# Two 128-column value products instead of three 64-column ones in a softmax attention branch, and eleven filler products left out

## Chip, cores and metric

One NeuronCore of a Trainium2 chip runs the whole program. The metric is the device time of one execution in microseconds (us). TensorE does the matrix products, VectorE (DVE), ScalarE (ACT) and GpSimd (POOL) the elementwise work; SyncE (SP) issues the large loads. All data are fp32; most products run on operands that were split into a high and a low part in the 32-bit matmul format (`F32R`).

## The reference, cut to what matters

Two transformer blocks on 512 tokens, width 1024. The first block mixes a retention branch with a softmax branch (`nsa`) of 8 query heads in 2 groups of keys and values, head width 64. The second block has two SwiGLU layers, a stick-breaking attention, a chunked softmax attention and a last gated projection.

```python
def nsa(q, kv_all, gate_logits, pos, ...):
    k_c, v_c, k_s, v_s, k_w, v_w = [kv[:, :, i] for i in range(6)]
    ...
        p_cmp = masked_softmax(s, cmp_end[None, :] <= tq[:, None])
        o_cmp = jnp.einsum('bghqn,bgnd->bghqd', p_cmp, vcT)          # compressed
        ...
        o_slc = jnp.einsum('bghqm,bgqmd->bghqd', p_slc, vg)          # selected
        ...
        o_win = jnp.einsum('bghqk,bgkd->bghqd', p_win, vwb)          # window
    o = g[..., 0:1] * o_cmp + g[..., 1:2] * o_slc + g[..., 2:3] * o_win
```

With 512 tokens the selection takes every block and the window covers all, so the selected and the window part are plain causal softmax attentions with keys and values of their own.

## The kernel before

**High and low parts.** A value a is kept as AH, its rounding to the matmul format, and AL = a - AH. `mm3` (lines 277 to 279) makes a product of two such values from three matmuls: high x low of the moving side, high x high, low x high. It takes three operand pairs and sums into one PSUM bank; the low x low part is left out.

**The softmax branch.** `NSA_UNITS` has 64 units: 8 heads, two kinds (selected, window) and 4 blocks of 128 queries, i = 0 to 3. A unit with block i sees (i + 1) blocks of 128 keys. `softmax_pairs` takes two units at a time (s = 0, 1; heads j and j + 4) in steps m, in the order of blocks 0, 3, 0, 3, 1, 2, 1, 2 for each head pair j, so 8 steps make a round and 4 rounds the branch. In step m TensorE does, in this order:

- the scores of pair m (L1646, three products per unit, the two units side by side in the upper and lower 64 rows) and the causal mask (L1720, a bf16 product with the identity),
- the transposes of the softmax weights of pair m - 3 (L1730), once GpSimd has scaled them (`sc`) and the bank is free (`lo` of the pair before),
- the value products of pair m - 4 into the banks B0 and B1 (`mm3`, L277 to L279): the values `VNH`, `VNL` (64 columns) are the loaded operand, the transposed weights `AH2`, `AL2` (128 columns) are streamed.

ScalarE takes the exponentials and rounds the transposed weights (`AH<-B`), VectorE takes the row maxima (L1248), the low parts (L1260) and reciprocals (L1266). A round collects one head pair in B0 and B1. At its end (m = 12, 20, 28, 36) ScalarE copies 64 rows of each bank to T10, T11 (event `at_x`, printed `T<-B 64x512`), and `nsa_first` begins the next round in the same banks with the compressed values `BD` (L1759), which waits for `at_x`. After two rounds (m = 20, 36) VectorE multiplies T10, T11 with the gate (`at_m`, L1273), ScalarE rounds (`at_hi`), VectorE takes the low part (`at_lo`, L1278).

**Behind it.** The output projection "p2" begins on TensorE right after the last value product; its weights are split on ScalarE (`KEPT_H`, L560) and VectorE (`KEPT_L`, L1021). In VectorE's queue some of these splits stand behind the `at_m` and `at_lo` of m = 36 and 37.

**Stick-breaking.** `stick_breaking(n)`, n = 4 to 38, is a pipeline over 32 units. At even n TensorE waits for a bank, runs `keep_clock` (L1528: matmuls of 128x512 on `VAH` whose result nobody reads), then the scores of two units (L1646); at every n it does the sums of later terms (`sb_later_sums`, L1866) once VectorE has made their low part, and the values of unit n - 7. `keep_clock` runs 10, 10 and 6 products at n = 4, 6 and 8, one at n = 10 to 30, and 6 at n = 32 and 34.

Of the kernel before, what the change touches and what calls it, by code (L numbers as in the profile page):

```python
# [17 lines left out]
P = 128  # L18
# [4 lines left out]
HD = 64  # L23
# [18 lines left out]
F32R = mybir.dt.float32r  # L42
# [22 lines left out]
def build(nc, a):  # L65
    with ExitStack() as ctx:
# [24 lines left out]
        def hb(name, kb, shape, dt=F32):  # L91
            return at(name, OFF_H + kb * KB, shape, dt)
# [8 lines left out]
        DECAY = hb("DECAY", 48, [P, NH, SEQ])  # L101
        QNH, QNL = hb("QNH", 64, [P, 4, SEQ], F32R), hb("QNL", 72, [P, 4, SEQ], F32R)
        KNH, KNL = hb("KNH", 80, [P, 2, SEQ], F32R), hb("KNL", 84, [P, 2, SEQ], F32R)
        VNH, VNL = hb("VNH", 88, [P, 4, 256], F32R), hb("VNL", 92, [P, 4, 256], F32R)
        Y_H = hb("Y_H", 48, [P, KT, SEQ])
        MRH, MRL = hb("MRH", 0, [P, 4, SEQ], F32R), hb("MRL", 8, [P, 4, SEQ], F32R)
        GR = hb("GR", 16, [P, 4, SEQ])
# [3 lines left out]
        W2K = hb("W2K", 52, [P, 2, 2, P])  # L111
        W2V = hb("W2V", 54, [P, 2, HD])
        HV4 = hb("HV4", 55, [P, 2, 2, 4, 32])
        BD = hb("BD", 57, [P, 2, 4, HD])
        KCF = hb("KCF", 59, [P, 4, 32])

        KPH, KPL = hb("KPH", 48, [P, 4, P], F32R), hb("KPL", 50, [P, 4, P], F32R)
        SCT = at("SCT", OFF_U + 4 * KB, [P, 2, SEQ])
# [172 lines left out]
            "pt_hi pt_lo pp ep pl_s".split())}  # L291


        pl_y, at_x, at_m, at_hi, at_lo = (Event(n) for n in "pl_y at_x at_m at_hi at_lo".split())
        f_g, f_s, f_u, f_h, f_hh, f_hl = (sem(n) for n in "f_g f_s f_u f_h f_hh f_hl".split())
        NSA = {n: Event("nsa_" + n) for n in "s max exp rec sc tr hi lo pv".split()}
        BAND = {n: Event("", NSA[n], 64) for n in "s max exp rec sc tr hi lo pv".split()}
# [59 lines left out]
        def nsa_unit(h, kind, i):  # L357
            g, j, L = h // 4, h % 4, (i + 1) * P
            rows, cols = slice(64 * g, 64 * g + 64), slice(i * P, (i + 1) * P)
            o = slice(kind * P + g * HD, kind * P + (g + 1) * HD)  # L360
            return {"h": h, "i": i, "L": L, "q": (QNH[rows, j, cols], QNL[rows, j, cols]),
                    "k": (KNH[rows, kind, 0:L], KNL[rows, kind, 0:L]), "mask": MASKB[:, 0, :], "bias": None,
                    "gate": GLS[:, i, 3 * h + kind + 1:3 * h + kind + 2],
                    "v": lambda b: (VNH[:, b, o], VNL[:, b, o])}

        def band_unit(h, i):
            L = (i + 1) * P
# [188 lines left out]
        def _(act):  # L556
# [100 lines left out]
            for d in range(32):  # L657
                if 4 <= d + 2 < 32:
                    hi_of_weights(d + 2)
                if d in ROT_DONE:  # L660
                    r = ROT_DONE[d]
                    wait(act, E["q_rot"], r + 1)
                    dst, scale = ROT_HI[r]
                    E["q_hi"].mark(f(dst, T[10][:, :], ACT.Copy, scale=scale))
                if d == 14:
                    wait(act, E["angle"], 2)
                    E["sines"].mark(f(T[2][:, :], T[3][:, :], ACT.Sin, scale=0.5))
                    wait(act, E["sines"], 3)
                    E["sines"].mark(f(T[3][:, :], T[3][:, :], ACT.Sin))
                act.wait_ge(mm, d + 1)  # L670
                kind = P1_KIND[d]
                bank = B[uses["p1", d][0]] if kind != TOK else None
                if kind == ROT:
                    wait(act, E["q_rot"], P1_ROT[d] - 3)
                    for q in range(4):
                        here, other = slice(32 * q, 32 * q + 32), slice(32 * (q ^ 1), 32 * (q ^ 1) + 32)
                        ins = f(Q_RING[P1_ROT[d] % 4][here, :], bank[other, :], ACT.Copy)
                    E["q_swap"].mark(ins)
                elif kind == GATE:
                    E["gates"].mark(f(RG[:, d // 16, d % 4, :], bank[:, :], ACT.Silu))  # L680
                elif kind == TOK and d % 4 == 3:
                    for t in range(TT):
                        if d < 16:
                            E["v_hi"].mark(f(VRH[:, t, :], B[4 + t][:, :], ACT.Copy))
                        else:
                            f(GLS[:, t, :], B[4 + t][:, 256:280], ACT.Sigmoid)
                            E["v_hi"].mark(f(VNH[:, t, :], B[4 + t][:, 0:256], ACT.Copy))


            for m in range(25):  # L690
# [198 lines left out]
            n = 0  # L889
# [121 lines left out]
        def _(dve):  # L1011
# [97 lines left out]
            for d in range(32):  # L1109
# [23 lines left out]
                if kind == CMP:  # L1133

                    dve.wait_ge(mm, d + 1)
                    kv = d - 20
                    bank = B[uses["p1", d][0]]
                    for g in range(2):
                        rows = slice(64 * g, 64 * g + 64)
                        tok = bank[rows, :].rearrange("p (n r) -> p r n", r=16)  # L1140
                        for l2 in range(2):
                            for part in range(2):
                                pe = PE2[rows, kv, 16 * part + l2:16 * part + 16:2]
                                ins = tt(FC[kv][64 * l2:64 * l2 + 64, 8 * part:8 * part + 8, g, :],
                                         tok[:, l2:16:2, part:part + NC],
                                         pe.unsqueeze(2).broadcast_to([64, 8, NC]), ALU.add)
                                E["k_flat"].mark(ins)
                elif kind == TOK and d % 4 == 3:
                    for t in range(TT):
                        wait(dve, E["v_hi"], (4 if d > 16 else 0) + t + 1)  # L1150
                        if d < 16:
                            E["v_lo"].mark(tt(VRL[:, t, :], B[4 + t][:, :], VRH[:, t, :], ALU.subtract))
                        else:
                            E["v_lo"].mark(tt(VNL[:, t, :], B[4 + t][:, 0:256], VNH[:, t, :], ALU.subtract))

            def compressed_keys_values():

                wait(dve, E["cmp_kv"], 1)
                for g in range(2):
                    rows = slice(64 * g, 64 * g + 64)  # L1160
                    tt(KCF[rows, 1, 0:NC], B[6][rows, g * NC:(g + 1) * NC], T[2][rows, NC:SEQ:16], ALU.mult)
                    chain.done(tt(KCF[rows, 2, 0:NC], B[6][rows, 64 + g * NC:64 + (g + 1) * NC], T[3][rows, NC:SEQ:16], ALU.mult))
                    chain.done(tt(KCF[rows, 0, 0:NC], KCF[rows, 1, 0:NC], KCF[rows, 2, 0:NC], ALU.add))
                for j in range(4):
                    cols = slice(32 * j, 32 * j + 32)
                    E["cmp_kh"].mark(v.tensor_copy(KPH[:, j, cols], KCF[:, 0, :]))
                wait(dve, E["cmp_kh"], 4)
                for j in range(4):
                    cols = slice(32 * j, 32 * j + 32)
                    E["cmp_kl"].mark(tt(KPL[:, j, cols], KCF[:, 0, :], KPH[:, j, cols], ALU.subtract))  # L1170
                for g in range(2):
                    for j in range(4):
                        rows = slice(32 * j, 32 * j + 32)
                        E["cmp_bd"].mark(v.tensor_copy(BD[rows, g, j, :], B[6][rows, P + HD * g:P + HD * (g + 1)]))


            dve.wait_ge(decay_here, 16)
            for m in range(26):
# [21 lines left out]
                if m == 17:  # L1200
# [3 lines left out]
                    v.memset(BD[:, :, :, :], 0.0)  # L1204
                    chain.done(v.memset(HV4[:, :, :, :, :], 0.0))
                    for KP in (KPH, KPL):
                        chain.done(v.tensor_copy(KP[:, :, :], BD[:, :, :, :].rearrange("p g j e -> p (g j e)").rearrange("p (j c) -> p j c", j=4)))
                    for hf in range(2):
                        src = HIDT[:, 1, hf, :].rearrange("p (g n) -> p g n", g=2).unsqueeze(2).broadcast_to([P, 2, 4, NC])
                        E["cmp_dup"].mark(v.tensor_copy(HV4[:, hf, :, :, 0:NC], src))  # L1210
# [55 lines left out]
                            tag["rec"].mark(v.reciprocal(RECS[:, u % 8:u % 8 + 1], SUMS[:, u % 8:u % 8 + 1]))  # L1266

            def nsa_ahead(m):
                if m in (20, 36):
                    for s in range(2):  # L1270
                        p = m // 36 + 2 * s
                        wait(dve, at_x, 4 * (m // 36) + 3 + s)
                        at_m.mark(tt(T[10 + s][:, :], T[10 + s][:, :], RG[:, 1, p, :], ALU.mult))  # L1273
                if m in (21, 37):
                    for s in range(2):
# [222 lines left out]
        def _(pe):  # L1498
# [209 lines left out]
            def softmax_pairs(units, tag, ahead, first):  # L1708

                N = len(units) // 2  # L1710
                for m in range(N + 4):
# [20 lines left out]
                    if m >= 4:  # L1732
                        for s in range(2):
# [3 lines left out]
                            started = first(m - 4, s)  # L1737
                            wait(pe, tag["lo"], u + 1)
                            for b in range(i + 1):
                                ins = mm3(B[s][0:HD, i * P:(i + 1) * P], *x["v"](b), AH2[:, u % 4, b * P:(b + 1) * P],  # L1740
                                          AL2[:, u % 4, b * P:(b + 1) * P], b == 0 and not started, b == i, skip_group_check=True)
                            tag["pv"].mark(ins)
# [12 lines left out]

            def nsa_first(m, s):
                if m % 8 == 0:
                    wait(pe, at_x, 2 * (m // 8 - 1) + s + 1)
                    mat(B[s][0:HD, :], BD[:, s, m // 8, :], PTC[:, s, :], start=True, stop=False, skip_group_check=True)  # L1759
                return True  # L1760

            wait(pe, E["gn_ln"], 4)
# [38 lines left out]
            def mlp_down(phase, d0, t, hidden):  # L1801
# [14 lines left out]
                for n in range(16):  # L1816
# [5 lines left out]
                    for k in range(FT - 16):  # L1822
# [8 lines left out]
            wait(pe, E["gn_lo"], 4)  # L1831
            project_out("p2", D_P2, 0, lambda k: MRH[:, k, :] if k < 4 else UH[:, k, :],
                        lambda k: MRL[:, k, :] if k < 4 else UL[:, k, :],
                        bank_free=lambda m: wait(pe, *((NSA["exp"], 62), (NSA["exp"], 62), (at_x, 7), (at_x, 8), (NSA["lo"], 64), (NSA["exp"], 64))[m]),
                        then=lambda: None,
                        ready=lambda k: wait(pe, at_lo, {4: 1, 5: 3, 6: 3, 7: 4}[k]))
            mlp_up("f1", D_F1, 0, 0)
# [80 lines left out]
            def stick_breaking(n):  # L1918
                if n < SB_ALONE and n % 2 == 0:
                    if n >= 8:  # L1920
                        wait(pe, E["sb_p"], n - 4)
                    else:
                        wait(pe, E["p5_vlo"], n + 2)
                    keep_clock({4: 10, 6: 10, 8: 6}.get(n, 1 if n < 32 else 6), VAH[:, 0, :], sb_bank(n))
                    if n < 32:
                        sb_scores(n)
                if SB_EARLY <= n - 3 < 32:
# [162 lines left out]
```

## Time and profile before

| | |
|---|---|
| time, median of 3 runs | 1579.76 us (1579.65 to 1583.11) |
| profiled execution: its own time | 1579.92 us |
| profiled execution: span | 1578.2 us |
| mean granted TensorE clock | 0.982 |
| TensorE busy | 1488.9 us (94%), 8593 matmuls |
| softmax branch, steady part | about 311 to 386 us |
| steady stick-breaking | about 972 to 1018 us |

The span is what the trace covers; the execution's own time lies 1.7 us above it. Busy time is a sum over instructions; matmuls overlap, so a busy TensorE can still be one that waits between short pieces. PEld is TensorE's loading of the operand that stays in the array. The granted clock is 1.00 at 2.4 GHz and 0.50 at 1.2 GHz. "Idle" in brackets is the time that an engine stood still just before an instruction, with what ended it.

### The profile page before, as it was taken

What the parts mean: (1) busy time and instruction counts of PE and PEld (TensorE: products, weight loads), DVE (VectorE), ACT (ScalarE), POOL (GpSimd) and SP (SyncE); (2) the same over time, 40 slices, a digit from 0 to 9 for tenths busy, and PEclk for the clock granted to TensorE, in tenths of its full rate; (3) what the DMA queues carried; (4) which work ended last, traced back from release to release, by engine and by line L of the source; (5) the groups of instructions that cost most, each with busy time, mean ns of one, the idle gap of its engine ahead of it and who ended that gap; (6) DMA issues with size and microseconds to landing.
All of it is one profiled execution on the core that took longest, in us unless ns stands there. A gap on an engine that the chain in (4) does not pass through costs nothing.

```text
span 1578.2 us, 22125 instructions
## 1 busy us (share of the span) xinstructions
PE 1488.9 (94%) x8593; PEld 1252.4 (79%) x8593; DVE 837.6 (53%) x1444; ACT 686.4 (43%) x1305; POOL 205.5 (13%) x309
## 2 busy tenths in 40 slices
PE   4999998999989999999989998988999999999997
PEld 2788866678988888888888886668988888888986
DVE  5767645577464444432275345875654444422364
ACT  4555535377443222322353235886542232222453
POOL 0000000144310000000130003653300000000211
PEclk9999999799999999999999999999999999999999
DMA  9533340002213333333403331003033333333321
GB/s 375 211 94 101 120 153 9 1 2 68 94 55 102 96 93 95 102 96 93 147 1 107 95 92 54 5 24 108 1 94 93 96 103 93 93 111 97 114 81 54
DMA packets 40531, 143.06 MB, mean 91 GB/s; under 512 B 4464, under 2 KB 6528, under 8 KB 39808
## 3 DMA queue, kind: packets, MB, share of 16 engines
q1 hardware_dynamic: 38240, 129.55, 25.8%
q0 software_dynamic: 1632, 11.52, 2.0%
q8 instruction: 55, 0.90, 0.2%
q10 hardware_dynamic: 576, 0.85, 0.2%
q14 instruction: 28, 0.23, 0.0%
HBM read 139.81 MB, written 2.10 MB: 90 GB/s over the span
## 4 chain that ended last, share of the span: by engine, by line
PE 81%; DVE 8%; ACT 5%; issue 3%; POOL 1%; DMA 1%; DVEq 0%; SPq 0%; POOLq 0%; ACTq 0%
PE B L277 24%; PE B L278 23%; PE B L279 23%; PE B L1646 3%; ACT T L560 2%; PE B L1730 1%; PE B L1528 1%; PE B L1866 1%; POOL T L480 1%; PE B L1625 1%; DVE WADA L1069 1%; DMA X<-in_x 1%; DVE WL L1023 1%; DVE KEPT_L L1021 1%; DVE X L1034 1%
## 5 line engine op out<-in xcount | busy, mean ns | idle before, releaser
L277 PE MATMUL B<-UH,WH 128*128 128x512 f32 (+1 forms) x1120 | 420.7, 376 | 17.1 <-DVE UL L1078 6.3
L278 PE MATMUL B<-UL,WH 128*128 128x512 f32 (+1 forms) x1120 | 417.0, 372 | 0.0
L279 PE MATMUL B<-UH,WL 128*128 128x512 f32 (+1 forms) x1120 | 416.9, 372 | 0.0
L277 PEld LDWEIGHTS B<-UH,WH 128*128 128x128 f32 x1120 | 212.1, 189 | 57.7 <-DVE UL L1041 7.6
L560 ACT ACTIVATE WH<-RAW 128x1024 fp32r<-128x1024 f32 x178 | 186.6, 1051 | 137.2 <-DMA RAW<-in_stream 117.0
L278 PEld LDWEIGHTS B<-UL,WH 128*128 128x128 f32 x1120 | 212.3, 190 | 36.3
L279 PEld LDWEIGHTS B<-UH,WL 128*128 128x128 f32 x1120 | 212.2, 189 | 36.4
L1023 DVE TENSOR_TENSOR WL<-RAW,WH 128x1024 fp32r<-128x1024 f32 x98 | 121.9, 1246 | 165.6 <-ACT WH L560 165.4
L560 ACT ACTIVATE T<-B 128x256 f32<-128x256 f32 (+3 forms) x207 | 96.0, 466 | 126.1 <-PE B L279 64.5
L1323 DVE TENSOR_TENSOR WL<-RAW,WH 128x1024 fp32r<-128x1024 f32 x80 | 98.1, 1226 | 76.7 <-ACT WH L560 74.0
L560 ACT ACTIVATE T<-T 128x512 f32<-128x512 f32 (+3 forms) x131 | 68.6, 525 | 134.2 <-DVE T L1327 119.2
L471 POOL TENSOR_TENSOR T<-T,T 128x256 f32<-128x256 f32 x60 | 52.7, 878 | 553.8 <-ACT T L560 552.9
L560 ACT ACTIVATE HH<-T 128x512 f32 (+1 forms) x44 | 27.8, 632 | 190.7 <-DVE T L1332 183.8
L277 PE MATMUL B<-HH,WH 128*128 128x512 f32 x256 | 99.6, 389 | 0.0
L278 PE MATMUL B<-HL,WH 128*128 128x512 f32 x256 | 99.6, 389 | 0.0
L279 PE MATMUL B<-HH,WL 128*128 128x512 f32 x256 | 99.6, 389 | 0.0
L1329 DVE TENSOR_TENSOR T<-B,T 128x512 f32<-128x512 f32 x40 | 27.7, 692 | 71.6 <-PE B L279 71.6
L277 PE MATMUL B<-UH,KEPT_H 128*128 128x256 f32 x192 | 54.8, 285 | 2.5 <-ACT T L560 2.5
L277 PE MATMUL B<-HH,TAIL_H 128*128 128x256 f32 x192 | 54.8, 286 | 1.7 <-ACT Y_U L560 1.7
L278 PEld LDWEIGHTS B<-HL,WH 128*128 128x128 f32 x256 | 48.1, 188 | 10.0
L279 PEld LDWEIGHTS B<-HH,WL 128*128 128x128 f32 x256 | 48.1, 188 | 10.0
L277 PEld LDWEIGHTS B<-HH,WH 128*128 128x128 f32 x256 | 48.1, 188 | 9.9
(340 smaller groups left out, 2928.9 us busy)
## 6 DMA issues: line engine op xcount, KB each, us to landing
RAW<-in_stream SPq DMA_DIRECT2D x202, 512.0 KB, 3.6
WADA<-in_w_ada SPq DMA_DIRECT2D x4, 2048.0 KB, 18.8
RAW<-in_stream SPq DMA_DIRECT2D x16, 384.0 KB, 3.2
WADA<-in_w_ada SPq DMA_DIRECT2D x4, 1024.0 KB, 18.4
W<-in_w POOLq DMA_DIRECT2D x2, 2048.0 KB, 11.3
X<-in_x SPq DMA_DIRECT2D x2, 1024.0 KB, 10.5
DECAY<-in_decay POOLq DMA_DIRECT2D x1, 2048.0 KB, 8.1
X<-in_x POOLq DMA_DIRECT2D x2, 1024.0 KB, 8.4
```

The costliest lines, as they stand in the source:

```text
L277: nc.tensor.matmul(out, lh, rh, start=start, stop=False, **kw)
L278: nc.tensor.matmul(out, lh, rl, start=False, stop=False, **kw)
L279: return nc.tensor.matmul(out, ll, rh, start=False, stop=stop, **kw)
L471: E["y_sum"].mark(nc.gpsimd.tensor_tensor(T[7][:, h], T[8][:, h] if k == 1 else T[7][:, h], T[8 + k % 2][:, h], ALU.add))
L480: E["n_sum"].mark(nc.gpsimd.tensor_tensor(T[4][:, h], T[2][:, h] if k == 1 else T[4][:, h], T[2 + k % 2][:, h], ALU.add))
L560: return nc.scalar.activation(out, in_, func, **kw)
L1021: tt(lo[:, :], RAW[:, d % SLOTS, 0:hi.shape[1]], hi[:, :], ALU.subtract).then_inc(w_lo, 1)
L1023: tt(WL[:, d % SLOTS, :], RAW[:, d % SLOTS, :], WH[:, d % SLOTS, :], ALU.subtract).then_inc(w_lo, 1)
L1034: E["x_new"].mark(stt(X[:, k, h], T_RING[k % 4][:, h], gain[:, k:k + 1], X[:, k, h], ALU.mult, ALU.add))
L1323: tt(WL[:, nxt, :], RAW[:, nxt, :], WH[:, nxt, :], ALU.subtract).then_inc(w_lo, 1)
L1329: tt(T[4][:, :], B[j][:, :], T[6][:, :], ALU.mult).then_inc(f_u, 1)
L1646: ins = [mat(outs[s], fixed[s][x], moving[s][y], start=(x + y == 0), stop=stop and x == 1) for s in range(2)]
```

## The change

The values of the softmax branch are laid out so that the high and the low part of one block stand side by side, 128 columns: `VN[:, block, kind and group, high or low, 64]`. A value product then takes two matmuls for each key block, both with this 128-column operand loaded: one streams `AL2`, one streams `AH2`. Rows 0 to 63 of the bank collect what the high values give, rows 64 to 127 what the low values give. `BD` gets 128 columns as well (the second 64 are zero), so that `nsa_first` begins all 128 rows. At a round's end ScalarE copies rows 0 to 63 as before, and VectorE adds rows 64 to 127 to the copy (new event `at_sum`); whoever waited for `at_x` now waits for `at_sum`. The product low x low is now included. In stick-breaking the eleven single `keep_clock` products at n = 10 to 30 are gone.

```diff
-        VNH, VNL = hb("VNH", 88, [P, 4, 256], F32R), hb("VNL", 92, [P, 4, 256], F32R)
+        VN = hb("VN", 88, [P, 4, 4, 2, HD], F32R)
...
-        BD = hb("BD", 57, [P, 2, 4, HD])
-        KCF = hb("KCF", 59, [P, 4, 32])
+        BD = hb("BD", 57, [P, 2, 4, P])
+        KCF = hb("KCF", 61, [P, 4, 32])
...
             def nsa_ahead(m):
+                if m >= 12 and (m - 12) % 8 == 0:
+                    j = (m - 12) // 8
+                    for s in range(2):
+                        rows = pair_rows(j)
+                        wait(dve, at_x, 2 * j + s + 1)
+                        at_sum.mark(tt(T[10 + s][rows, :], B[s][HD:P, :], T[10 + s][rows, :], ALU.add))
                 if m in (20, 36):
                     for s in range(2):
                         p = m // 36 + 2 * s
-                        wait(dve, at_x, 4 * (m // 36) + 3 + s)
+                        wait(dve, at_sum, 4 * (m // 36) + 3 + s)
...
                             for b in range(i + 1):
+                                if units is NSA_UNITS:
+                                    at = slice(b * P, (b + 1) * P)
+                                    mat(B[s][:, i * P:(i + 1) * P], x["both"](b), AL2[:, u % 4, at],
+                                        start=False, stop=False, skip_group_check=True)
+                                    ins = mat(B[s][:, i * P:(i + 1) * P], x["both"](b), AH2[:, u % 4, at],
+                                              start=False, stop=b == i, skip_group_check=True)
+                                    continue
                                 ins = mm3(B[s][0:HD, i * P:(i + 1) * P], *x["v"](b), AH2[:, u % 4, b * P:(b + 1) * P],
...
-                    wait(pe, at_x, 2 * (m // 8 - 1) + s + 1)
-                    mat(B[s][0:HD, :], BD[:, s, m // 8, :], PTC[:, s, :], start=True, stop=False, skip_group_check=True)
+                    wait(pe, at_sum, 2 * (m // 8 - 1) + s + 1)
+                    mat(B[s][:, :], BD[:, s, m // 8, :], PTC[:, s, :], start=True, stop=False, skip_group_check=True)
...
-                    keep_clock({4: 10, 6: 10, 8: 6}.get(n, 1 if n < 32 else 6), VAH[:, 0, :], sb_bank(n))
+                    keep_clock({4: 10, 6: 10, 8: 6}.get(n, 0 if n < 32 else 6), VAH[:, 0, :], sb_bank(n))
```

On TensorE, the value products of one unit with block 2 in the second round (three key blocks, into B0). The names are output <- streamed, loaded; the number pair is loaded columns x streamed columns. Before:

```order
L277 MATMUL B0<-AH2_79,VNH_72 64x128
L278 MATMUL B0<-AL2_80,VNH_72 64x128
L279 MATMUL B0<-AH2_79,VNL_73 64x128
L277 MATMUL B0<-AH2_79,VNH_72 64x128
L278 MATMUL B0<-AL2_80,VNH_72 64x128
L279 MATMUL B0<-AH2_79,VNL_73 64x128
L277 MATMUL B0<-AH2_79,VNH_72 64x128
L278 MATMUL B0<-AL2_80,VNH_72 64x128
L279 MATMUL B0<-AH2_79,VNL_73 64x128
```

And in the changed kernel:

```order
L1747 MATMUL B0<-AL2_79,VN_72 128x128
L1749 MATMUL B0<-AH2_78,VN_72 128x128
L1747 MATMUL B0<-AL2_79,VN_72 128x128
L1749 MATMUL B0<-AH2_78,VN_72 128x128
L1747 MATMUL B0<-AL2_79,VN_72 128x128
L1749 MATMUL B0<-AH2_78,VN_72 128x128
```

Nine matmuls that load 64 columns each became six that load 128 each; the streamed columns of one stay 128.

On VectorE, the changed kernel at a round's end, m = 12 (names as above, the event waited for in brackets):

```order
L1265 RECIPROCAL RECS<-SUMS 128x1 [waits nsa_exp] x2
L1273 TENSOR_TENSOR T_171<-B,T_171 64x512 [waits at_x]
L1273 TENSOR_TENSOR T_172<-B,T_172 64x512 [waits at_x]
L1247 TENSOR_REDUCE NMAX<-B 128x1 [waits nsa_s] x2
L1259 TENSOR_TENSOR AL_79<-B,AH_78 128x512 [waits nsa_hi] x2
```

The two rows with `at_x` are new; before, the maxima of step 12 followed the reciprocals of step 11 directly. At m = 36 the same two stand ahead of the gate products and of the last splits of the projection's weights:

```order
L1273 TENSOR_TENSOR T_171<-B,T_171 64x512 [waits at_x]
L1273 TENSOR_TENSOR T_172<-B,T_172 64x512 [waits at_x]
L1278 TENSOR_TENSOR T_171<-T_171,RG 128x512 [waits at_sum]
L1278 TENSOR_TENSOR T_172<-T_172,RG 128x512 [waits at_sum]
L1283 TENSOR_TENSOR UL<-T_171,UH 128x512 [waits at_hi]
L1283 TENSOR_TENSOR UL<-T_172,UH 128x512 [waits at_hi]
L1020 TENSOR_TENSOR KEPT_L_134<-RAW,KEPT_H_133 128x1024 [waits w_hi]
```

What moved: everything from the gate products on stands two additions later in VectorE's queue.

## Rows read from the trace of the kernel before

**Rows 1.** Windows, one round each: span, busy (count) by engine, PEclk, DMA.

```profile
326.00:347.30 21.30, 21.16 (x230) 16.77 (x230) 14.79 (x48) 15.38 (x51) 9.59 (x17) 1.00 0.01 2
```

**Rows 2.** Waits of TensorE and the chain's shares, 311 to 386 us.

```profile
PE B L1730 <- DVE AL L1260: 0.5, 1, 0.5
by line: PE B L1646 21.0%; PE B L1730 20.3%; PE B L277 11.0%; PE B L279 10.0%; PE B L278 10.0%; PE B L1759 8.0%; PE B L1720 7.0%; DVE AL L1260 5.1%; ACT AH L560 2.8%; issue 2.0%; DVE KEPT_L L1021 1.5%; ACT KEPT_H L560 1.3%; DVE RECS L1266 0
```

**Rows 3.** Timeline of PEld: the 18 loads of one pair's value products.

```profile
319.56 0.14 PEld L277 LDWEIGHTS B<-AH,VNH 128*64 128x64 f32 x1
319.67 0.14 PEld L278 LDWEIGHTS B<-AL,VNH 128*64 128x64 f32 x1
319.73 0.14 PEld L279 LDWEIGHTS B<-AH,VNL 128*64 128x64 f32 x1
...
320.64 0.13 PEld L279 LDWEIGHTS B<-AH,VNL 128*64 128x64 f32 x1
320.85 0.19 PEld L1646 LDWEIGHTS B<-KNH,QNH 64*128 64x128 f32 x2
```

**Rows 4.** Groups by tile and line: duration ns min/median/max, first and last start.

```profile
L277 PEld LDWEIGHTS B<-AH,VNH x160: 132/135/138, 306.7 to 386.4; 128*64 128x64 f32 x160
L1866 PEld LDWEIGHTS B<-SPH,TRI x72: 186/188/331, 940.0 to 1022.4; 128*128 128x128 f32 x72
L1720 PEld LDWEIGHTS B<-MASKB,IDB x96: 95/98/118, 294.3 to 1065.4; 128*128 128x128 bf16 x96
L1528 PEld LDWEIGHTS B<-QNH x40: 187/188/332, 283.5 to 293.3; 128*128 128x128 f32 x40
L1204 DVE MEMSET BD<- x1: 485/485/485, 260.4 to 260.4; 128x512 f32 x1
```

**Rows 5.** Timeline in stick-breaking: two 128-column loads, the matmul between.

```profile
987.99 0.22 PE L1866 MATMUL B<-SPH,TRI 128*128 128x128 f32 x1
987.99 0.19 PEld L1866 LDWEIGHTS B<-SPL,TRI 128*128 128x128 f32 x1
...
988.10 0.14 PEld L277 LDWEIGHTS B<-AH,VAH 128*64 128x64 f32 x1
```

**Rows 6.** Windows, one period of steady stick-breaking (columns as in rows 1).

```profile
987.00:1002.70 15.70, 14.34 (x93) 10.40 (x93) 13.98 (x33) 14.24 (x36) 10.62 (x24) 1.00 0.00 1
```

**Rows 7.** Chain of work in order of time, from the branch into p2.

```profile
387.16 0.60 ACT T L560
387.78 0.70 DVE T L1273
...
391.75 0.36 PE B L277
```

**Rows 8.** Timelines at the rounds' ends, m = 20 and m = 12.

```profile
347.58 1.07 ACT L560 ACTIVATE T<-B 64x512 f32<-64x512 f32 x2
...
348.28 0.19 PEld L1759 LDWEIGHTS B<-PTC,BD 128*64 128x64 f32 x2 [0.17 <-ACT T L560]
...
326.16 1.06 ACT L560 ACTIVATE T<-B 64x512 f32<-64x512 f32 x2
327.00 1.07 PE L1759 MATMUL B<-PTC,BD 128*64 128x512 f32 x2
```

**Rows 9.** Waits, 388 to 393 us.

```profile
PE B L277 <- DVE KEPT_L L1021: 0.6, 1, 0.6
```

**Rows 10.** Timeline of VectorE in the retention stage.

```profile
264.84 0.69 DVE L1199 TENSOR_TENSOR GM<-GM,GR 128x512 f32<-128x512 f32 x1 [1.32 <-ACT GR L560]
```

**Rows 11.** Chain of work in order of time: one single filler product on it.

```profile
991.94 0.23 PE B L1528
```

**Rows 12.** Timeline: ScalarE behind that filler product.

```profile
992.87 0.62 ACT L560 ACTIVATE AH<-T 128x512 fp32r<-128x512 f32 x1
993.52 1.08 ACT L560 ACTIVATE T<-T 128x384 f32<-128x384 f32 x2
```

**Rows 13.** Windows around the start of stick-breaking (columns as in rows 1).

```profile
965.00:970.00 5.00, 5.00 (x25) 4.18 (x25) 2.48 (x7) 2.55 (x7) 1.61 (x3) 0.66 0.00 0
```

More of the change, by code:

```diff
@@ L291, in build @@
             "pt_hi pt_lo pp ep pl_s".split())}
-        pl_y, at_x, at_m, at_hi, at_lo = (Event(n) for n in "pl_y at_x at_m at_hi at_lo".split())
+        pl_y, at_x, at_sum, at_m, at_hi, at_lo = (Event(n) for n in "pl_y at_x at_sum at_m at_hi at_lo".split())
         f_g, f_s, f_u, f_h, f_hh, f_hl = (sem(n) for n in "f_g f_s f_u f_h f_hh f_hl".split())
@@ L359, in nsa_unit @@
             rows, cols = slice(64 * g, 64 * g + 64), slice(i * P, (i + 1) * P)
-            o = slice(kind * P + g * HD, kind * P + (g + 1) * HD)
             return {"h": h, "i": i, "L": L, "q": (QNH[rows, j, cols], QNL[rows, j, cols]),
@@ L363, in nsa_unit @@
                     "gate": GLS[:, i, 3 * h + kind + 1:3 * h + kind + 2],
-                    "v": lambda b: (VNH[:, b, o], VNL[:, b, o])}
+                    "both": lambda b: VN[:, b, 2 * kind + g, :, :]}
         def band_unit(h, i):
@@ L686, in _ @@
                             f(GLS[:, t, :], B[4 + t][:, 256:280], ACT.Sigmoid)
-                            E["v_hi"].mark(f(VNH[:, t, :], B[4 + t][:, 0:256], ACT.Copy))
+                            E["v_hi"].mark(f(VN[:, t, :, 0, :], B[4 + t][:, 0:256].rearrange("p (c e) -> p c e", c=4), ACT.Copy))
             for m in range(25):
@@ L1153, in _ @@
                         else:
-                            E["v_lo"].mark(tt(VNL[:, t, :], B[4 + t][:, 0:256], VNH[:, t, :], ALU.subtract))
+                            E["v_lo"].mark(tt(VN[:, t, :, 1, :], B[4 + t][:, 0:256].rearrange("p (c e) -> p c e", c=4), VN[:, t, :, 0, :], ALU.subtract))
             def compressed_keys_values():
@@ L1173, in compressed_keys_values @@
                         rows = slice(32 * j, 32 * j + 32)
-                        E["cmp_bd"].mark(v.tensor_copy(BD[rows, g, j, :], B[6][rows, P + HD * g:P + HD * (g + 1)]))
+                        E["cmp_bd"].mark(v.tensor_copy(BD[rows, g, j, 0:HD], B[6][rows, P + HD * g:P + HD * (g + 1)]))
             dve.wait_ge(decay_here, 16)
@@ L1206, in _ @@
                     for KP in (KPH, KPL):
-                        chain.done(v.tensor_copy(KP[:, :, :], BD[:, :, :, :].rearrange("p g j e -> p (g j e)").rearrange("p (j c) -> p j c", j=4)))
+                        chain.done(v.tensor_copy(KP[:, :, :], BD[:, 0, :, :]))
                     for hf in range(2):
@@ L1833, in _ @@
                         lambda k: MRL[:, k, :] if k < 4 else UL[:, k, :],
-                        bank_free=lambda m: wait(pe, *((NSA["exp"], 62), (NSA["exp"], 62), (at_x, 7), (at_x, 8), (NSA["lo"], 64), (NSA["exp"], 64))[m]),
+                        bank_free=lambda m: wait(pe, *((NSA["exp"], 62), (NSA["exp"], 62), (at_sum, 7), (at_sum, 8), (NSA["lo"], 64), (NSA["exp"], 64))[m]),
                         then=lambda: None,
```

## The prediction

> **What bounds the kernel now.** Two places matter, the softmax branch and steady stick-breaking. For the branch I first took the windows, one round each: TensorE is busy 21.16 of 21.30 us at the full clock, VectorE 14.79, ScalarE 15.38 [rows 1]. Busy time can hide waits, so the next views are the waits and the chain's shares: TensorE has one wait of 0.5 us in 75 us, and its lines make up 87% of the chain (21.0 + 20.3 + 11.0 + 10.0 + 10.0 + 8.0 + 7.0) [rows 2]. The branch goes at TensorE's own pace; what a product costs there is paid in full.
>
> What is that pace? The timeline of the loads shows it: within the value products one load starts 0.06 us after the other (319.67, 319.73), 18 loads and the change to the next scores take 320.85 - 319.56 = 1.29 us [rows 3]. A load of 64 columns is recorded with 135 ns, one of 128 columns in the matmul format with 186 to 188 ns, some 53 ns more [rows 4]. The durations overlap, so the slot must be read from starts: in stick-breaking a 128-column load begins at 987.99 together with a 128-column stream, and the next load only at 988.10, 0.11 us later [rows 5]. A stream of 128 columns alone takes no more than the 0.06 us [rows 3] of before. So with 128 streamed columns the load sets the pace: 0.06 us for 64 loaded columns, 0.11 us for 128.
>
> Steady stick-breaking is bound by a loop over all engines: in a period of 15.70 us ScalarE is busy 14.24, VectorE 13.98, TensorE 14.34 [rows 6], and the chain runs through each in turn.
>
> **The change part by part.**
>
> *Value products.* 160 key blocks [rows 4] had three products and get two: 3 x 0.06 = 0.18 us against 2 x 0.109 = 0.22 us, 0.038 us more each, 6.1 us in all if nothing else changed. The ends of a run save some of it. A run of n products now takes 0.11 (the first load still waits for the last transpose) + (n - 2) x 0.06 + 0.21 us; n = 18 gives 1.28, measured 1.29 [rows 3]. With k = 2n/3 products of 0.109 us it is (k - 1) x 0.109 + 0.26, the last term being the 0.21 us plus the longer last load. For n = 6, 12, 18, 24 this gives 0.59, 1.02, 1.46, 1.90 against 0.56, 0.92, 1.28, 1.64: +0.03, +0.10, +0.18, +0.26, together 0.57 us. Each occurs twice in a round, four rounds: **+4.5 us**. The last two pairs (0.3 us) run beside the chain of the round's end below, so +4.2 us count.
>
> The Trainium skill (TensorE: Matmul & The Clock Gate, section Back-to-back issue gap) gives about 81 ns for a pair of load and matmul with 128 streamed columns in a sustained stream. By that, 320 products would take 25.9 us where 480 at 60 ns take 28.8: -2.9 us. Neither 60 ns nor 110 ns of this trace is 81 ns, and the sum above goes by the rows.
>
> *Compressed products.* Their load gets 128 columns. It is hidden under 512 streamed columns except the first of each of eight: at most 8 x 0.05 = +0.4 us. I take **+0.3 us**.
>
> *The addition at a round's end.* No row has it; the nearest is a VectorE product of 128x512 at 0.70 us [rows 7], ScalarE's 64x512 copy takes 0.6 us [rows 7]; I take 0.65 us. TensorE waits for the first of the two before `nsa_first`. At m = 20 the copy begins at 347.58, ends some 0.6 us later, and TensorE starts at 348.28: 0.1 us of slack; at m = 12 it is 327.00 - 326.76 = 0.24 us [rows 8]. Slack grows by the 0.18 us that the 18 products between take longer. So the wait is 0.65 - 0.28 = 0.37 us once and 0.65 - 0.42 = 0.23 us twice (m = 28 repeats 12): 0.8 us. Queued behind the additions on VectorE are the maxima, the low parts and reciprocals of that step, 1.3 us later. VectorE has 6.5 us free in a round [rows 1] and TensorE does 2 us of compressed products meanwhile; only at m = 20, where the gate products stand behind too, do the next transposes wait, about 0.2 us. **+1.0 us**, between 0 and +2.5.
>
> *The end of the branch.* Here VectorE leads. The chain goes from the copy (387.16) over the gate product (387.78), ScalarE's rounding, the low parts and one weight split to TensorE at 391.75 [rows 7], which waits 0.6 us for it [rows 9]. There is no slack: two additions ahead of the gate products push all of it back by 2 x 0.65 = **+1.3 us**. TensorE fills none of it, since its queue is in order.
>
> *Clearing `BD`* takes 0.49 us [rows 4] and doubles; it runs in the retention stage, just ahead of a 1.32 us wait of VectorE for ScalarE [rows 10], which takes it in. If that cover were gone it would cost 0.5 us. The values' new layout changes strides only: 0.
>
> *Filler products.* Eleven of 0.23 us [rows 11], 2.5 us at most. Nine lie on the chain, but ScalarE stands right behind: after the filler at 991.94 it finishes one operation at 993.49 and starts the exponentials of the scores at 993.52, so it could not have begun earlier [rows 12]. With 1.5 us of idle ScalarE in a period [rows 6] part of the 0.23 us must come back. I take 0.4 of 2.5: **-1.0 us**, between 0 and -2.5.
>
> Sum: 4.2 + 0.3 + 1.0 + 1.3 - 1.0 = +5.8 us on the profiled execution's own 1579.9 us, which is 0.2 us above the median: 1585.6 us.
>
> **The rivals.**
>
> *A. Wide loads are as quick as narrow ones* (ends on the other side). If the second product of a block needs no new load, or a 128-column load fits under 128 streamed columns, the pace stays 0.06 us: 160 x 0.06 = -9.6 us, -9.6 + 1.0 + 1.3 - 1.0 = -8.3, so 1571.5 us. It decides once the slot falls below 0.09 us. For it: the mask's load, 128 columns in bf16, takes 98 ns [rows 4], so wide loads can be quick. Against it: the same width in the matmul format takes 188 ns, the 40 filler products on one operand have 40 loads [rows 4], and the 0.11 us [rows 5] follow a load of the very operand that was in place. The Trainium skill (TensorE: Matmul & The Clock Gate, Weight-path perf modes) says that the fast load is on for 128 columns of any type but FP32; whether `F32R` counts as FP32 is what this rival hangs on. The 186 ns against 98 ns speak against it here. Half of it is possible too: a slot of 0.08 us, between the two that the rows show, gives 320 x 0.08 - 480 x 0.06 = -3.2 us and, with the other terms, -3.2 + 0.3 + 1.0 + 1.3 - 1.0 = -1.6, 1578.3 us: no change that can be told. The 81 ns of the skill's section above would mean this case.
>
> *B. The clock falls.* In the value products the array streams half the time instead of nearly all of it, and stick-breaking loses its fillers. The clock did fall in this program: 0.66 in the window at 965 us, just behind a thin stretch of stick-breaking [rows 13], while the branch is at 1.00 now. A stretch of 3.4 us at 1.2 GHz (what 0.66 over 5 us makes) loses about 1.2 us in the branch, where some two thirds of TensorE's time is streaming. One in each round: +5 us, 1590.5 us.
>
> *C. Less comes through.* The additions hide in VectorE's free time but for the branch's end, and the fillers come back nearly whole: 4.2 + 0.1 + 0.3 + 1.3 - 2.2 = +3.7, 1583.5 us.
>
> **How the numbers follow.** A measurement of this kernel tells 0.3%, 4.7 us, from no change, so the bound lies at 1584.5. The forecast has 0.48, A 0.08 and its half 0.04, B 0.13, C 0.27. Faster is A alone, 0.08; same is C and A's half, 0.31; slower is the forecast and B, 0.61. The likeliest case's own range is 1583 to 1588.5. Bounds of the costs: all low, 4.2 + 0 + 0 + 1.2 - 2.5 = +2.9; all high, 6.1 + 0.4 + 2.5 + 1.5 - 0 = +10.5, 1590.3; with part of B on it 1592. Outside stay A, its half and the worst of B, some 0.2 together. The range is 1579 to 1592.
>
> **What would show it.** Right: loads of `VN` at 186 to 190 ns and starting 0.11 us apart; a round of 22.6 to 23.0 us instead of 21.3; TensorE waiting 0.2 to 0.4 us ahead of the compressed products, on VectorE; the gap at the entry to p2 at 1.5 to 2 us; VectorE's new 64x512 additions at 0.6 to 0.7 us; the period of stick-breaking between 15.1 and 15.7 us. Wrong: loads of `VN` every 0.06 us (A), a granted clock below 1.00 between 310 and 386 us or between 970 and 1020 us (B), a period near 15.1 us (C).

## The result, and the profile after

| | before | changed |
|---|---|---|
| median, 11 runs of each in turn on one chip | 1580.81 us (1579.24 to 1583.45) | 1585.92 us (1584.07 to 1587.54) |
| ratio, 95% interval | | 1.0031 (1.0022 to 1.0039) |
| profiled execution: its own time, span | 1579.92, 1578.2 us | 1585.78, 1584.0 us |

The changed kernel is slower by 5.1 us. That is just above the 0.3% that I had taken as the bound; the whole interval lies above 1. The page's summary of the changed kernel:

```profile
span 1584.0 us, 21791 instructions
PE 1492.4 (94%) x8422; PEld 1259.8 (80%) x8422; DVE 843.1 (53%) x1452; ACT 685.5 (43%) x1305; POOL 204.4 (13%) x309
```

TensorE has 171 matmuls fewer (160 + 11) and is busy 3.5 us longer. The value products' loads, by tile and line:

```profile
L1747 PEld LDWEIGHTS B<-AL,VN x160: 186/192/293, 305.9 to 391.1; 128*128 128x128 f32 x160
L1749 PEld LDWEIGHTS B<-AH,VN x160: 189/192/192, 306.4 to 391.2; 128*128 128x128 f32 x160
```

And the timeline of loads for the twelve products of the pair whose 18 loads are [rows 3]:

```profile
319.65 0.19 PEld L1747 LDWEIGHTS B<-AL,VN 128*128 128x128 f32 x1
319.76 0.19 PEld L1749 LDWEIGHTS B<-AH,VN 128*128 128x128 f32 x1
...
320.88 0.19 PEld L1749 LDWEIGHTS B<-AH,VN 128*128 128x128 f32 x1
321.14 0.19 PEld L1651 LDWEIGHTS B<-KNH,QNH 64*128 64x128 f32 x2
```

The loads start 0.11 us apart. From the first load to the next scores it takes 1.49 us where it took 1.29, +0.20 us; +0.18 was forecast.

The windows, the second and third round, and two halves of steady stick-breaking (columns as in [rows 1]):

```profile
328.00:350.70 22.70, 22.22 (x189) 18.51 (x189) 16.03 (x51) 15.62 (x51) 9.57 (x16) 1.00 0.01 1
350.70:374.00 23.30, 22.57 (x189) 18.56 (x190) 18.45 (x55) 16.61 (x54) 10.56 (x16) 1.00 0.01 1
...
979.60:994.80 15.20, 13.46 (x90) 9.76 (x90) 13.49 (x32) 13.87 (x35) 10.27 (x24) 1.00 0.01 2
994.80:1010.10 15.30, 13.52 (x91) 9.84 (x92) 14.05 (x33) 14.19 (x37) 10.72 (x25) 1.00 0.00 1
```

A round takes 22.7 and 23.3 us instead of 21.3 [rows 1], and TensorE now stands still for 0.5 to 0.7 us of it. The clock is 1.00 in all four stretches. A period of stick-breaking takes 15.2 to 15.3 us instead of 15.7 [rows 6]. A lower clock stands between 970 and 1020 us too, ahead of these two halves:

```profile
970.00:975.00 5.00, 3.52 (x13) 3.18 (x14) 3.68 (x8) 3.52 (x7) 2.20 (x4) 0.66 0.00 0
```

It is the fall of [rows 13], around the fillers of n = 8, which start at 973.23 us here and at 966.55 before.

The waits, 303 to 400 us, name what TensorE stands still for (total, times, longest), at the rounds' ends and at the entry to the projection:

```profile
PE B L1771 <- DVE T L1273: 0.9, 3, 0.4
PE B L277 <- DVE KEPT_L L1020: 1.6, 1, 1.6
```

The 0.6 us of [rows 9] have become 1.6. The chain of work there, in order of time:

```profile
391.63 0.60 ACT T L559
392.25 1.31 DVE T L1273 x2
393.59 0.70 DVE T L1278
394.31 0.64 ACT UH L559
394.98 1.30 DVE UL L1283 x2
396.27 1.15 DVE KEPT_L L1020
397.42 0.14 issue
397.56 0.36 PE B L277
```

Against [rows 7] one link is new, the two additions with 1.31 us. From the copy's start to TensorE it took 4.59 us and takes 5.93, +1.34.

At m = 20 the additions cost more than TensorE's wait for them. VectorE's timeline:

```profile
349.85 1.30 DVE L1273 TENSOR_TENSOR T<-B,T 64x512 f32<-64x512 f32 x2 [1.00 <-ACT T L559]
351.18 1.29 DVE L1278 TENSOR_TENSOR T<-T,RG 128x512 f32<-128x512 f32 x2
352.51 0.76 DVE L1247 TENSOR_REDUCE NMAX<-B 128x1 f32<-128x256 f32 x2
353.18 1.28 DVE L1259 TENSOR_TENSOR AL<-B,AH 128x512 fp32r<-128x512 f32 x2
```

It idles 1.00 us for the copy, and then additions and gate products, 2.6 us, stand ahead of the maxima that the next exponentials need. ScalarE waits:

```profile
ACT T L559 <- DVE NMAX L1247: 1.6, 1, 1.6
```

One thing I had not expected is in the loads at this place: the compressed products of both units with the value products of the first between them. A row with x2 holds both loads of a compressed product, and its time is that of the first.

```profile
350.60 0.30 PEld L1771 LDWEIGHTS B<-PTC,BD 128*128 128x128 f32 x2 [0.62 <-DVE T L1273]
...
351.56 0.19 PEld L1749 LDWEIGHTS B<-AH,VN 128*128 128x128 f32 x1 [0.24 <-issue]
351.67 0.30 PEld L1771 LDWEIGHTS B<-PTC,BD 128*128 128x128 f32 x2
```

A unit of a compressed product and its first value products takes 351.67 - 350.60 = 1.07 us. The same unit of the kernel before, at the places of [rows 8]:

```profile
328.32 0.19 PEld L1759 LDWEIGHTS B<-PTC,BD 128*64 128x64 f32 x2
...
349.28 0.13 PEld L277 LDWEIGHTS B<-AH,VNH 128*64 128x64 f32 x1 [0.81 <-issue]
...
349.39 0.14 PEld L279 LDWEIGHTS B<-AH,VNL 128*64 128x64 f32 x1
349.60 0.19 PEld L1759 LDWEIGHTS B<-PTC,BD 128*64 128x64 f32 x2
```

With the first of the pair at 327.00 and at 348.28 [rows 8] it took 1.32 us, although every load in it is shorter. The first value product's load began only 1.00 us after that of `BD` (349.28). So part of what the value products cost is paid back here, though I had booked a small loss.

### The profile page after: what moved, and what is told of

Its sections match the earlier page's. It is cut to its first block, busy times and chain, and to the rows that moved or that the text cites. A ratio compares the mean times of both kernels' runs of the same rounds, so it can differ in the third digit from the quotient of the medians.

```text
span 1584.0 us, 21791 instructions
## 1 busy us (share of the span) xinstructions
PE 1492.4 (94%) x8422; PEld 1259.8 (80%) x8422; DVE 843.1 (53%) x1452; ACT 685.5 (43%) x1305; POOL 204.4 (13%) x309
## 4 chain that ended last, share of the span: by engine, by line
PE 79%; DVE 7%; ACT 6%; issue 4%; POOL 3%; DMA 1%; SPq 0%; DVEq 0%; POOLq 0%; ACTq 0%
PE B L277 23%; PE B L279 22%; PE B L278 22%; PE B L1651 2%; ACT T L559 2%; PE B L1735 1%; PE B L1533 1%; PE B L1749 1%; POOL T L479 1%; PE B L1747 1%; PE B L1630 1%; DVE WADA L1068 1%; DMA X<-in_x 1%; DVE WL L1022 1%; PE B L1878 1%
```

## The experiments

The theory to begin with was the forecast's: value products +4.2 us, additions +2.3, fillers -1.0, compressed products about nothing. The rival reading: the value products cost less than that, or the fillers gave nothing, and the additions make up the rest. All ratios are to the kernel before, run in turn on the same chip: its median was 1580.81 us (27 runs) for the first four, 1580.22 (20 runs) for the next two and 1581.57 (9 runs) for the last.

**1. The kernel before without the eleven fillers.**

```diff
-                    keep_clock({4: 10, 6: 10, 8: 6}.get(n, 1 if n < 32 else 6), VAH[:, 0, :], sb_bank(n))
+                    keep_clock({4: 10, 6: 10, 8: 6}.get(n, 0 if n < 32 else 6), VAH[:, 0, :], sb_bank(n))
```

> The kernel before with the eleven single filler products of stick-breaking left out, nothing else. Theory 1 (they lie on the loop and most of their time comes back): 1.8 us less than before, as the changed kernel's stick-breaking drifted against the old one, ratio about 0.9989. Theory 2 (ScalarE bounds the loop, as I had reckoned): 1.0 us less or nothing. Theory 3 (the clock falls without them): a granted clock below 1.00 between 970 and 1020 us and no gain.

Measured: 1580.23 us, ratio 0.9996 (0.9987 to 1.0005), not to be told from no change. Its windows, one period (as [rows 6]) and all of it:

```profile
990.10:1005.30 15.20, 13.43 (x90) 9.75 (x92) 13.94 (x33) 14.06 (x36) 10.61 (x25) 1.00 0.01 2
...
970.00:1020.00 50.00, 44.80 (x291) 33.03 (x291) 44.19 (x100) 43.36 (x107) 33.91 (x76) 1.00 0.00 1
```

The period is 15.20 instead of 15.70, as in the changed kernel, and the clock stays at 1.00 over all 50 us with TensorE busy for 44.80 of them. From the scores of n = 8 to the first value product of the chunked attention it took 61.7 us instead of 63.3, -1.6. The chunked attention itself then took 0.45 us longer from its first to its last value product. It took 0.3 to 0.5 us longer in the changed kernel and in experiments 4 and 6 too, but not in experiment 5; why, no run tells. The trace gives -1.2 us net, the medians -0.6, with an interval from -2.1 to +0.8.

**2. The changed kernel with the fillers back.** The same line with a 1 in place of the 0.

> The changed kernel with the eleven single filler products back: the softmax branch's part of the change alone. Theory 1: 1.8 us above the changed kernel, 7 us above before (ratio 1.0045), since branch and stick-breaking do not touch each other. Theory 2: 1.0 us or less above the changed kernel.

Measured: 1586.28 us, ratio 1.0041 (1.0028 to 1.0055), 0.4 us above the changed kernel by the medians and 1.6 by the ratios, from five runs; the whole times do not size the fillers. From n = 8 to the chunked attention it is 63.3 us again, the rounds are as in the changed kernel within 0.05 us. So the two parts of the change don't touch each other, and the loss is all in the branch.

**3. The kernel before with the wide `BD` alone.**

```diff
-        BD = hb("BD", 57, [P, 2, 4, HD])
-        KCF = hb("KCF", 59, [P, 4, 32])
+        BD = hb("BD", 57, [P, 2, 4, P])
+        KCF = hb("KCF", 61, [P, 4, 32])
...
-                    mat(B[s][0:HD, :], BD[:, s, m // 8, :], PTC[:, s, :], start=True, stop=False, skip_group_check=True)
+                    mat(B[s][:, :], BD[:, s, m // 8, :], PTC[:, s, :], start=True, stop=False, skip_group_check=True)
```

> The kernel before with BD alone widened to 128 columns (second half zero), three 64-column value products as before. Theory 1 (in the changed kernel's trace a unit with a compressed product takes 1.08 instead of 1.33 us, because with both loads 128 wide the next load starts while the long stream still runs): if the width of BD alone does it, 8 x 0.25 = 2.0 us less than before. Theory 2 (what counts is that both loads have the same width; here 128 is followed by 64 and 64 by 128): 0 to 0.4 us more than before. Theory 3 (the saving came from the wait on the addition ahead of it): no change.

Measured: 1579.07 us, ratio 0.9986 (0.9977 to 0.9995): 2.2 us faster by the ratio (0.8 to 3.6), 1.7 by the medians, from a load that is longer. The timeline of its loads:

```profile
348.38 0.30 PEld L1759 LDWEIGHTS B<-PTC,BD 128*128 128x128 f32 x2
348.92 0.14 PEld L277 LDWEIGHTS B<-AH,VNH 128*64 128x64 f32 x1 [0.24 <-issue]
...
349.41 0.13 PEld L279 LDWEIGHTS B<-AH,VNL 128*64 128x64 f32 x1
349.47 0.30 PEld L1759 LDWEIGHTS B<-PTC,BD 128*128 128x128 f32 x2
```

The load of `VNH` starts 0.54 us after that of `BD` instead of 1.00, while the compressed product still streams, and the unit takes 1.09 us instead of 1.32. With 8 such units that is 8 x 0.23 = 1.8 us. The load of `BD` itself also comes sooner, 0.06 us after the one of `VNL` ahead of it (349.41, 349.47) where it was 0.21 (349.39, 349.60).

**4. The changed kernel without the additions.** The low values' part is left out of the result.

```diff
-                        at_sum.mark(tt(T[10 + s][rows, :], B[s][HD:P, :], T[10 + s][rows, :], ALU.add))
...
-                    wait(pe, at_sum, 2 * (m // 8 - 1) + s + 1)
+                    wait(pe, at_x, 2 * (m // 8 - 1) + s + 1)
```

> The changed kernel without the eight additions on VectorE; those who waited for them wait for the copy again. The low values' share of the output is left out. Theory 1 (the additions cost about 1 us at the rounds' ends inside and 1.3 us at the branch's end): 2.3 us less than the changed kernel, the gap at the entry to p2 back from 1.6 to about 0.4 us. Theory 2 (VectorE's free time hides them): less than 0.5 us less.

Measured: 1582.15 us, ratio 1.0009 (1.0000 to 1.0018), 3.8 us below the changed kernel by the medians, 3.5 by the ratios, where 2.3 were expected. Its second round by the windows, and its only wait at the entry to the projection:

```profile
328.50:350.50 22.00, 21.89 (x190) 18.43 (x190) 14.30 (x47) 15.33 (x51) 9.57 (x16) 1.00 0.01 1
```

```profile
PE B L277 <- DVE KEPT_L L1020: 0.3, 1, 0.3
```

The round takes 22.0 us, with TensorE busy for all but 0.1, and by the starts of the compressed products the third takes as long. The third round loses the most by the additions, 23.3 - 22.0 = 1.3 us; it begins with the step m = 20 shown above.

**5. The changed kernel with narrow loads.** Both value products load the 64 high columns only; the low values are left out.

```diff
-                    "both": lambda b: VN[:, b, 2 * kind + g, :, :]}
+                    "both": lambda b: VN[:, b, 2 * kind + g, 0, :]}
...
-                                    mat(B[s][:, i * P:(i + 1) * P], x["both"](b), AL2[:, u % 4, at],
+                                    mat(B[s][0:HD, i * P:(i + 1) * P], x["both"](b), AL2[:, u % 4, at],
```

> The changed kernel with both value products loading only the 64 columns of high values instead of 128; BD stays 128 wide, the additions stay (they add zeros). The low values are left out of the product. Theory 1 (the width of the load sets the slot, 0.11 against 0.06 us): loads 0.06 us apart, 320 x 0.052 = 16 us less than the changed kernel, less some 1 to 4 us where other engines then bound the rounds; about 1571 us. Theory 2 (the number of products or the chain over the other engines sets the pace): less than 3 us less.

Measured: 1575.70 us, ratio 0.9971 (0.9960 to 0.9982), 10.2 us below the changed kernel by the medians, 9.5 by the ratios. The loads and TensorE's waits, 306 to 392 us:

```profile
319.39 0.14 PEld L1749 LDWEIGHTS B<-AH,VN 128*64 128x64 f32 x1
319.45 0.14 PEld L1747 LDWEIGHTS B<-AL,VN 128*64 128x64 f32 x1
```

```profile
PE B L1735 <- DVE AL L1259: 2.6, 9, 0.7
PE B L1771 <- DVE T L1273: 2.3, 3, 0.9
PE B L277 <- DVE KEPT_L L1020: 2.3, 1, 2.3
```

The same matmuls with the same streamed columns go in slots of 0.06 us once the load has 64 columns. So it is the width of the load that costs 0.05 us for each product, and not the order of the products. A product writes as many rows of the bank as it has loaded columns, so no run parts these two. 320 x 0.05 = 16 us would come of it, and about 10 do. TensorE now waits 2.6 + 2.3 + 2.3 = 7.2 us for VectorE, where the two waits shown of the changed kernel are 2.5; that is 4.7 of the missing 6, and the rest was not traced. The expected 1571 us was almost 5 us too low.

**6. The kernel before with the wide `BD` and without the fillers** (the edits of 1 and 3).

> The kernel before with BD widened to 128 columns and without the eleven single filler products, value products as before. If both savings that the changed kernel's trace shows hold by themselves and add up: 2.0 + 1.8 = 3.8 us less than before, ratio 0.9976. If the width of BD saves nothing beside 64-column products: 1.8 us less, ratio 0.9989.

Measured: 1578.05 us, ratio 0.9983 (0.9974 to 0.9991). It beats both kernels, the one before by 2.7 us by the ratio (1.4 to 4.1) and 2.2 by the medians. That is about the sum of what experiments 1 and 3 gave by their ratios, 0.6 + 2.2, and less than the 3.8 that was expected. Its second round:

```profile
325.00:345.90 20.90, 20.76 (x230) 17.08 (x229) 14.31 (x47) 15.46 (x51) 9.58 (x16) 1.00 0.01 2
```

Experiments 4 and 6 both have the wide `BD`, no fillers and no additions; only the value products differ. The rounds are 22.0 against 20.9 us. Timelines from the first compressed load to the projection's first product, experiment 4 and then 6:

```profile
306.31 0.30 PEld L1765 LDWEIGHTS B<-PTC,BD 128*128 128x128 f32 x2
...
389.81 0.33 PE L277 MATMUL B<-MRH,KEPT_H 128*128 128x256 f32 x1
```

```profile
304.00 0.30 PEld L1759 LDWEIGHTS B<-PTC,BD 128*128 128x128 f32 x2
...
383.32 0.33 PE L277 MATMUL B<-MRH,KEPT_H 128*128 128x256 f32 x1
```

83.50 against 79.32 us: up to there the value products alone cost 4.2 us. The wait for `KEPT_L` just behind gives 0.3 us of it back, being 0.3 us in experiment 4 and 0.6 in experiment 6: 3.9 us net. The whole runs give 0.0026 of 1580.5, 4.1 us, by the ratios, and 3.5 by the medians, each against its own kernel before.

**7. What keeps the loads apart?** Two readings of experiment 3 were left. (a) The change between a 64-column product in fp32 and 64-column products in the matmul format holds the next load back. (b) Any long stream through 64 loaded columns does. In the kernel before, `BD` and `PTC` are rounded to the matmul format and stay 64 wide; the low parts of that product are left out.

```diff
-        PTC = hb("PTC", 48, [P, 2, SEQ])
+        PTC = hb("PTC", 48, [P, 2, SEQ], F32R)
...
-        BD = hb("BD", 57, [P, 2, 4, HD])
+        BD = hb("BD", 57, [P, 2, 4, HD], F32R)
```

> The kernel before with the compressed product's two operands in the rounded matmul format, BD still 64 columns wide, so that it is one pass of 512 columns instead of two at half pace; the low parts of this product are left out. Before, a load behind this product began only 0.52 us after its second half (0.09 us after the stream's end), with BD 128 wide it begins while the stream runs. Theory 1 (it is the switch between a 64-column fp32 product and 64-column products in the matmul format that keeps the loads apart): now the next load starts 2 to 5 ns after the start of the 512-column stream, and a unit with its compressed product takes about 0.22 + 0.18 = 0.40 us instead of 1.33, 7 us less than before in all. Theory 2 (any 512-column stream from 64 loaded columns keeps the next load away until it ends): the next load starts 0.3 us after the start of the stream, a unit takes about 0.55 to 0.7 us, 5 us less than before.

Measured: 1575.57 us, ratio 0.9965 (0.9952 to 0.9978), 5.5 us faster by the ratio and 6.0 by the medians. That lies between what the two readings had asked for, 7 and 5 us, so the loads have to tell. The loads at the same place:

```profile
347.01 0.13 PEld L1760 LDWEIGHTS B<-PTC,BD 128*64 128x64 f32 x1
347.06 0.14 PEld L277 LDWEIGHTS B<-AH,VNH 128*64 128x64 f32 x1
...
347.49 0.13 PEld L1760 LDWEIGHTS B<-PTC,BD 128*64 128x64 f32 x1
```

The value product's load starts 0.05 us after that of `BD`, under the stream of 512 columns, and the unit takes 0.48 us. A long stream through 64 columns does not hold the next load back, so (b) is refuted.

(a) is what is left of the two, and it is not shown by itself: this run takes the fp32 product away altogether, so a third reading, (c), stands beside it, that a 64-column product in fp32 holds back whatever comes behind it. Two things speak for (a). In the kernel before, the load of `BD` is itself late behind `VNL`, 0.21 us where the wide `BD` has 0.06, though no fp32 stream runs then. And the two loads of one compressed product are not held apart: together they take 0.19 us (349.60), with some 0.14 us for one. In experiment 3 the type changes just as here, with 128 columns on the fp32 side, and the next load starts under the stream; so the type alone is not enough, it takes fp32 with 64 loaded columns. A kernel with two different 64-column fp32 products in a row would decide between (a) and (c).

The Trainium skill (TensorEngine Tiling (Array Packing), Key Properties) says that a change of tiling mode drains TensorE. Between the kernel before and this one the type alone changed, with 128 rows and 64 columns on both sides, so that page of the Trainium skill does not name this case.

## Why the prediction was right, and which terms were not

The forecast was 1585.6 us and the measured median 1585.9, the profiled execution 1585.8 for 1585.6. The change itself was forecast at +5.8 us and is +5.1 by the medians. The forecast stood on 1579.8 us for the kernel before, whose median beside the changed kernel was 1580.8; that brings the two absolute times closer together than the two differences. The terms:

| term | forecast | measured | from |
|---|---|---|---|
| value products | +4.2 | +3.9 (trace), +4.1 (ratio), +3.5 (medians) | experiments 4 and 6 |
| compressed products | +0.3 | -1.7 (medians), -2.2 (ratio) | experiment 3 |
| additions at rounds' ends | +1.0 | +2.5 (medians), +2.2 (ratios) | 3.8 or 3.5 (experiment 4) less the next row |
| end of the branch | +1.3 | +1.3 | chain of the changed kernel |
| clearing `BD` | 0 | 0 | not tried by itself |
| fillers | -1.0 | -1.2 (trace), -0.6 (medians) | experiment 1 |
| sum | +5.8 | +3.6 to +5.6 | +5.1 measured |

- **Value products: right in mechanism and size.** The slot of 0.11 us read from [rows 5] is the slot of the new loads, and a run of twelve took 1.49 us for 1.46. Experiment 5 shows that the load's width sets it. By the trace it is 4.2 us up to the projection and 3.9 behind its wait, for 4.5 and 4.2 forecast.
- **Compressed products: the step that failed.** I reasoned that the load is hidden under 512 streamed columns, so that width could only cost. That is not what a compressed product did in the kernel before: the next load waited for the end of its stream and came 1.00 us after that of `BD`. The longer load does away with that wait, which is worth 0.23 us a unit and 1.7 to 2.2 us in all. The rows for it stand in the trace of before; I read [rows 8] for the wait ahead of the product and not for what followed it. The sign was wrong, by 2.0 to 2.5 us.
- **Additions: the waits were right, the queue behind them was not.** The three waits ahead of the compressed products were forecast at 0.8 us in sum and are 0.9. What I had put at 0.2 us, and is 1.3 to 1.6, is the queue behind the additions at m = 20. It is the larger one because VectorE cannot start them before ScalarE's copy has ended, idles 1.00 us for it, and has the gate products next; then ScalarE is late by 1.6 us and with it the transposes. Free time of VectorE over a round does not help a step in which its queue is full. The third round, 23.3 us, lies outside the 22.6 to 23.0 that I had named. The term's upper bound of 2.5 us held, just.
- **End of the branch: right**, 1.34 us for 1.3. This was the one place where VectorE led already, so a delay could be added up link by link.
- **Fillers: more came back than I had reckoned.** In stick-breaking it is 1.6 of the 2.5 us, not 1.0. ScalarE, which I had taken for the limit behind the filler [rows 12], is not on the chain right behind any filler: the chain goes from the filler over the scores to VectorE or on along TensorE. The trace shows 0.45 us given back behind stick-breaking; net, the -1.0 is met within what can be measured.

The errors of the second and the third row, some -2.3 and +1.5, took each other out for the most part. The agreement to 0.3 us is luck in that part, and in the level of the kernel before. The sum of the measured terms cannot test the forecast any closer than the 2.0 us between its bounds.

The profiled executions differ by 5.9 us, more than the medians. One stretch holds some of it: in the output projection the changed kernel's clock fell for a moment where that of the kernel before did not. The windows there, before and changed:

```profile
459.00:463.00 4.00, 4.00 (x32) 3.91 (x31) 1.56 (x3) 2.72 (x4) 0.00 (x0) 1.00 0.47 138
```

```profile
459.00:463.00 4.00, 3.42 (x14) 3.15 (x15) 2.01 (x5) 1.60 (x4) 0.85 (x1) 0.58 0.00 0
```

From the first product behind the wait for `KEPT_L` (391.75 [rows 7]; 397.56) to the first value product of stick-breaking (966.23; 972.91) it took 574.5 us before and 575.4 in the changed kernel; an estimate of the fall's price from these is 0.9 us. Experiment 1 has such a fall there too, without any of the branch's edits, as have 2, 4 and 5; experiments 3, 6 and 7 have none. So it is not shown to belong to the change.

The rivals: A is refuted by the loads, 0.11 us apart, and by experiment 5, in which the 0.06 us that it wanted did need narrow loads. Its half-way slot of 81 ns from the Trainium skill (TensorE: Matmul & The Clock Gate, Back-to-back issue gap) is not found either: this kernel has 60 ns with 64 loaded columns and 110 ns with 128. The same page of the Trainium skill (Weight-path perf modes) leaves FP32 out of the fast load; the trace agrees if `F32R` counts as FP32, with 192 ns against 98 ns for bf16. B is refuted by the clock, 1.00 in every window shown of the branch and of steady stick-breaking. The 0.66 at 970 us is inside the stretch that I had named as B's sign, but it is the fall that the kernel before has as well, moved along with the fillers of n = 8, 6.7 us later; experiment 2, which has the fillers, shows 0.66 in the same window. C is refuted in its first half, since the additions were not hidden. Its sign for the fillers, a period near 15.1 us, all but came, but what arrived is 1.6 us and not 2.2.

## What to carry to other kernels

Merging products into wider ones pays by slots, not by count: here three matmuls with 64 loaded columns (0.18 us) beat two with 128 (0.22 us), since with 128 streamed columns the load sets the pace; read the slot from the starts of loads, never from their durations. A product in fp32 between narrow products of the matmul format is worth a look at the load that follows it: loading it 128 wide, the rest zeros, gained 1.7 to 2.2 us here. New work on an engine with free time costs nothing only where its queue has room at that step, so price it where it waits for its input and where something urgent stands behind it.

## What was not expected of the hardware

- After a product in fp32 with 64 loaded and 512 streamed columns, the next load of a 64-column operand in the matmul format began 1.00 us after the first one of the fp32 operand. It was 0.54 us with 128 loaded columns, and 0.05 us with 64 columns and both in the matmul format. The unit took 1.32, 1.09 and 0.48 us. What holds the load back, the change or the fp32 product with 64 columns by itself, is open.
- The longer load therefore made the kernel faster, in an engine that is 94% busy: busy time held waits between streams that no row named otherwise than as "issue".
